# The router's product computed from transposed residual rows, between the w_o products

## What is computed

```python
x = x + gate1[:, None, :] * mix                          # mix = merged @ w_o
h = modulate(rms_norm(x, norm2_w[l]), shift2, scale2)    # (rms_norm(x) * w) * (1 + scale2) + shift2
ffn = moe_ffn(h, w_router[l], b_router[l], ...)
# in moe_ffn:
logits = (hf @ w_router + b_router).astype(jnp.float32)
top_vals, top_idx = lax.top_k(logits, TOP_K)
top_w = jax.nn.softmax(top_vals, axis=-1)
```

## Time and profile before

| | |
|---|---|
| time, three runs | 2203.03 us median (2201.9 to 2205.33) |
| time of the profiled execution | 2187.63 us |
| span of the profiled execution | 2185.8 us |
| TensorE busy | 2038.8 us (93%), 16673 instructions |
| VectorE busy | 810.2 us (37%) |
| ScalarE busy | 264.8 us (12%) |
| GpSimd busy | 155.1 us (7%) |
| mean granted TensorE clock | 0.971 |
| bytes moved | 563.70 MB, mean 258 GB/s |

### The profile page before, as it was taken

The page is one execution under the profiler, slowest core; times in us unless marked ns, Lnnn a source line. Parts: engine busy times, 40 slices in busy tenths (PEclk is TensorE's granted clock), DMA queues, the critical chain, the costliest instruction groups (busy, mean ns, idle before and its releaser), DMA issues.

```text
span 2185.8 us, 42419 instructions
## 1 busy us (share of the span) xinstructions
PE 2038.8 (93%) x16673; PEld 980.1 (45%) x16673; DVE 810.2 (37%) x1887; ACT 264.8 (12%) x585; POOL 155.1 (7%) x219
## 2 busy tenths in 40 slices
PE   6999999999979999998899999999999999999970
PEld 3564556455644444445343444444444444434430
DVE  1666886687663000043221221221221222222216
ACT  2122112112121000010100100100100100100000
POOL 0011111111110000011200000000000000000002
PEclk9999999999989999996999999999999999999995
DMA  9463333333124222436999999999999999999934
GB/s 316 124 187 119 113 116 93 94 115 96 53 73 144 77 77 67 138 136 240 305 413 404 407 407 402 407 411 405 403 410 403 404 406 406 409 405 403 410 136 179
DMA packets 199129, 563.70 MB, mean 258 GB/s; under 512 B 15181, under 2 KB 135025, under 8 KB 146357
## 3 DMA queue, kind: packets, MB, share of 16 engines
q1 hardware_dynamic: 176431, 528.12, 63.7%
q0 software_dynamic: 6624, 21.77, 2.9%
q10 hardware_dynamic: 16038, 13.32, 1.9%
HBM read 537.62 MB, written 25.54 MB: 258 GB/s over the span
## 4 chain that ended last, share of the span: by engine, by line
PE 48%; DVE 1%; POOL 1%; DMA 1%; issue 0%; ACTq 0%; ACT 0%; POOLq 0%; DVEq 0%
PE ps L1730 30%; PE ps L1752 16%; PE ps L1739 1%; PE ps L1717 1%; POOL ring L616 1%; DVE ring L1400 1%; POOL slot_tok L603 0%; DMA yT<-slot_tok 0%; DMA slot_tok<-tid,slotki 0%; DVE yT L1406 0%; DVE yT L1404 0%; DVE ring L1403 0%; ACTq L851 0%; ACT zs L896 0%; DVE ring L1397 0%
## 5 line engine op out<-in xcount | busy, mean ns | idle before, releaser
L1730 PE MATMUL ps<-ring,hT 128*32 128x512 f32 x6336 | 690.9, 595 | 1.1 <-ACT hT L865 1.1
L1417 PE MATMUL ps<-hT,ring 128*128 128x512 f32 x1008 | 440.4, 595 | 0.0
L1730 PEld LDWEIGHTS ps<-ring,hT 128*32 128x32 f32 x6336 | 203.4, 110 | 461.4 <-issue 457.5
L1752 PE MATMUL ps<-ring,seg 128*32 128x256 f32 x6336 | 348.7, 380 | 3.4 <-ACT seg L874 3.4
L1315 DVE TENSOR_TENSOR hT<-ps,bgu 128x512 f32<-128x512 f32 x99 | 67.9, 686 | 627.2 <-PE ps L1730 627.2
L1417 PEld LDWEIGHTS ps<-hT,ring 128*128 128x128 f32 x1008 | 191.1, 191 | 231.2 <-issue 230.6
L1752 PEld LDWEIGHTS ps<-ring,seg 128*32 128x32 f32 x6336 | 202.5, 110 | 137.5 <-ACT seg L874 3.6
L1018 DVE SCALAR_TENSOR_TENSOR c<-ring,pcur,c 128x512 f32<-128x512 f32 x232 | 155.5, 744 | 0.0
L857 ACT ACTIVATE mm<-hT 128x256 f32<-128x256 f32 x99 | 45.2, 457 | 694.8 <-DVE hT L1317 694.8
L1417 PE MATMUL ps<-yT,ring 128*128 128x512 f32 x256 | 111.2, 592 | 1.0 <-ACT yT L723 1.0
L1417 PE MATMUL ps<-ring,hT 128*128 128x256 f32 x512 | 111.8, 379 | 0.0
(11 more groups left out here) (258 smaller groups left out, 1327.6 us busy)
## 6 DMA issues: line engine op xcount, KB each, us to landing
ring<-in_w_gate_up_dram SPq DMA_DIRECT2D x264, 1024.0 KB, 8.8
ring<-in_w_down_dram SPq DMA_DIRECT2D x132, 1024.0 KB, 7.8
ring<-in_w_ada_dram SPq DMA_DIRECT2D x24, 1024.0 KB, 8.7
ring<-in_w_in_dram SPq DMA_DIRECT2D x48, 512.0 KB, 4.1
ring<-in_w_in_dram SPq DMA_DIRECT2D x16, 1024.0 KB, 5.4
item_rows<-zs ACTq DMA_DIRECT2D x132, 96.0 KB, 5.2
ring<-decay_rows SPq DMA_DIRECT2D x8, 1024.0 KB, 7.2
ring<-in_w_ssm_out_dram SPq DMA_DIRECT2D x8, 1024.0 KB, 5.5
```

The source lines that it names most:

```text
L1417: last = T.matmul(out_, lhs(k), rhs(k), start=(k == 0), stop=(k == n - 1))
L1730: last = T.matmul(ps[j * GT:(j + 1) * GT, g, :], xT[:, k, g * GT:(g + 1) * GT], gu[:, k, j * GUW:(j + 1) * GUW], start=(k == 0), stop=(k = ...
L1752: last = T.matmul(ps[j * GT:(j + 1) * GT, 3 + g // 2, (g % 2) * DW:(g % 2 + 1) * DW], hidT[:, k % 2, g, k // 2, :], dn[:, k, j * DW:(j + 1 ...
```

## The change

The router's product is no longer made from the normalised rows. The norm's weight and scale are per column of the width, so they are folded into the router's weights: `wra[k] = wr[k] * norm2_w * (1 + scale2)`. The shift gives a constant row, `shift2 @ wr`, which is added to `b_router` once. The factor `rstd` of each token is applied to the logits when VectorE reads them. So the transposes can take `x2` before its norm (`turn_x2`).

The product itself has the 32 router columns as stationary operand and 128 tokens moving, in four 32-column tiles (`router_parts`): tile j sums two of the eight blocks of the width. ScalarE copies the result to `lpart`, and one matmul with `sum4` (ones at a stride of 32) sums the four parts and turns them back to tokens by experts (`router_sum`). These steps and the rank products stand between the w_o products. The w_o products rotate over three banks in place of four.

For the folding, three loads (`wr`, moved from after the last `branch_a`, and two new ones of scale, shift and norm weight in rows, `mrows`) stand on SP's queue behind `load_branches(1)`. TensorE waits for them and transposes `mrows` behind `branch_b(0)`; VectorE builds `wra` and `wrs` behind `merge(0)`; TensorE computes the constant row behind the last branch product.

ScalarE's order changes: for each t it now does the two copies of the transposes, the copy of `lpart`, and then the Square; before, all four Squares stood ahead of all copies. VectorE's order is written out: residual 0, norm 0, residual 1, route 0, norm 1, residual 2, route 1, norm 2, residual 3, route 2, norm 3, route 3.

```diff
@@ SP
             load_branches(1)
+            sp.dma_start(wr, w_router[0].rearrange("(k p) n -> p k n", p=P)).then_inc(once_in, 16)
+            sp.dma_start(mrows[0:2 * KT, :], mod_rows[3 * KT:5 * KT, :]).then_inc(once_in, 16)
+            sp.dma_start(mrows[2 * KT:, :], norm2_w[0].rearrange("(k n) -> k n", n=P)).then_inc(once_in, 16)
             with sp.Fori(2, KT) as m:
...
             sp.dma_start(x2, x_v).then_inc(x2_in, 16)
-            sp.dma_start(wr, w_router[0].rearrange("(k p) n -> p k n", p=P)).then_inc(once_in, 16)
@@ ScalarE
             for t in range(TT):
+                act.wait_ge(x2T_pe, t + 1)
+                if t >= 2:
+                    act.wait_ge(lp_pe, t - 1)
+                for b in range(2):
+                    nc.scalar.activation(x2T[:, t % 2, 4 * b:4 * b + 4, :].rearrange("p k n -> p (k n)"), ps[:, 4 + b, :],
+                                         ACT.Copy).then_inc(x2T_ok, 1)
+                act.wait_ge(lp_pe, t + 1)
+                if t >= 2:
+                    act.wait_ge(lg_pe, t - 1)
+                nc.scalar.activation(lpart[:, t % 2, :], ps[:, 6, 0:P], ACT.Copy).then_inc(lp_ok, 1)
                 act.wait_ge(x2_ok, 4 * (t + 1))
                 if t:
                     act.wait_ge(sq_ok, TT + t)
                 nc.scalar.activation(orow, x2[:, t, :], ACT.Square, accum_out=ss[:, t:t + 1]).then_inc(sq_ok, 1)
-            for t in range(TT):
-                act.wait_ge(h2T_pe, t + 1)
-                if t >= 2:
-                    act.wait_ge(lg_pe, t - 1)
-                for b in range(2):
-                    nc.scalar.activation(h2T[:, t % 2, 4 * b:4 * b + 4, :].rearrange("p k n -> p (k n)"), ps[:, 4 + b, :],
-                                         ACT.Copy).then_inc(h2T_ok, 1)
@@ VectorE
             merge(0)
+            dve.wait_ge(prT_ok, 4)
+            V.tensor_copy(as2[:, 0:KT], ps[:, 6, 2 * KT:3 * KT]).then_inc(par_ok, 1)
+            V.tensor_copy(as2[:, KT:2 * KT], ps[:, 6, 0:KT]).then_inc(par_ok, 1)
+            dve.wait_ge(par_ok, 19)
+            V.scalar_tensor_tensor(as2[:, 0:KT], ps[:, 6, KT:2 * KT], 1.0, as2[:, 0:KT], ALU.add, ALU.mult).then_inc(par_ok, 1)
+            dve.wait_ge(par_ok, 20)
+            V.tensor_tensor(wra, wr, as2[:, 0:KT].unsqueeze(2).to_broadcast([P, KT, NE]), ALU.mult).then_inc(par_ok, 1)
+            V.tensor_tensor(wrs, wr, as2[:, KT:2 * KT].unsqueeze(2).to_broadcast([P, KT, NE]), ALU.mult).then_inc(par_ok, 1)
             with dve.Fori(1, KT) as m:
                 merge(m)
+            dve.wait_ge(prT_ok, 5)
+            V.tensor_tensor(brow[:, :], brow[:, :], ps[:, 6, 64:64 + NE], ALU.add).then_inc(par_ok, 1)
...
+            def route(t):
+
                 dve.wait_ge(lg_pe, t + 1)
-                link(V.tensor_tensor(lg[:, t, :], ps[:, LG_BANK[t], 0:NE], brow[:, :], ALU.add))
+                dve.wait_ge(rstd_ok, t + 2)
+                dve.wait_ge(par_ok, 23)
+                link(V.scalar_tensor_tensor(lg[:, t, :], logits(t), rstd[:, t:t + 1], brow[:, :], ALU.mult, ALU.add))
...
+            second_residual(0)
+            second_norm(0)
+            second_residual(1)
+            route(0)
+            second_norm(1)
+            second_residual(2)
+            route(1)
+            second_norm(2)
+            second_residual(3)
+            route(2)
+            second_norm(3)
+            route(3)
@@ TensorE
             branch_a(0, first=True)
             branch_b(0, first=True)
+            pe.wait_ge(once_in, 64)
+            T.transpose(ps[:, 6, 0:3 * KT], mrows, ident[0:3 * KT, 0:3 * KT]).then_inc(prT_ok, 1)
...
+            def turn_x2(t):
+                pe.wait_ge(x2_ok, 4 * (t + 1))
...
+            def router_parts(t):
+                pe.wait_ge(x2T_ok, 2 * t + 2)
...
+                for a in range(2):
+                    for j in range(4):
+                        last = T.matmul(ps[32 * j:32 * j + 32, 6, 0:P], wra[:, 2 * j + a, :], x2T[:, t % 2, 2 * j + a, :],
+                                        start=(a == 0), stop=(a == 1))
+                last.then_inc(lp_pe, 1)
+
+            def router_sum(t):
+                pe.wait_ge(lp_ok, t + 1)
...
+                T.matmul(logits(t), lpart[:, t % 2, :], sum4[:, :], start=True, stop=True).then_inc(lg_pe, 1)
...
+            pe.wait_ge(par_ok, 22)
+            for k in range(KT):
+                last = T.matmul(ps[:, 6, 64:64 + NE], ones[:, :], wrs[:, k, :], start=(k == 0), stop=(k == KT - 1))
+            last.then_inc(prT_ok, 1)
             pe.wait_ge(wo_in, 16)
             pe.wait_ge(mrg_ok, 3 * KT)
...
+            project_o(0, 0)
+            project_o(0, 1)
+            project_o(1, 0)
+            turn_x2(0)
+            project_o(1, 1)
+            router_parts(0)
+            project_o(2, 0)
+            router_sum(0)
+            turn_x2(1)
+            project_o(2, 1)
+            router_parts(1)
+            project_o(3, 0)
+            router_sum(1)
+            turn_x2(2)
+            rank_own(0)
+            project_o(3, 1)
+            router_parts(2)
+            rank_before(1)
+            rank_own(1)
+            router_sum(2)
+            turn_x2(3)
+            router_parts(3)
+            rank_before(2)
+            rank_own(2)
+            rank_before(3)
+            router_sum(3)
+            rank_own(3).then_inc(rank_pe, 1)
+            for j in range(TT):
+                last = T.matmul(ps[:, 4, 0:NE], ones[:, :], mask[:, j, :], start=(j == 0), stop=(j == TT - 1))
             last.then_inc(rank_pe, 1)
```

More of the change, by code:

```diff
@@ L232, in build @@
         wr = state[:, :, :].rearrange("p a b -> p (a b)").rearrange("p (k n) -> p k n", k=KT)
+        wra = ytmp[:, :].rearrange("p (k n) -> p k n", k=KT)
+        wrs = sqj[:, :].rearrange("p (k n) -> p k n", k=KT)
+        mrows = xb[0:3 * KT, 0, 0:P]
+        as2 = sb("as2", [P, 2 * KT])
+        sum4 = sb("sum4", [P, NE])
+        lpart = seg[:, :, 0, :]
         brow = sb("brow", [P, NE])
@@ L1221, in second_norm, with second_residual @@
                 V.tensor_tensor(h2[:, t, :], h2[:, t, :], s2row, ALU.add).then_inc(h2_ok, 1)
-            for t in range(TT):
+            def second_residual(t):
                 for hf in range(2):
                     n = 2 * t + hf
+                    cols = slice(hf * 512, (hf + 1) * 512)
                     dve.wait_ge(o_pe, n + 1)
@@ L1504, in _ @@
             for t in range(TT):
-                last = T.matmul(ps[:, 4, t * H:(t + 1) * H], dt_part[:, ch(t)], dt_sum, start=True, stop=True)
+                last = T.matmul(ps[:, 4, t * H:(t + 1) * H], dt_part[:, ch(t)], sum4[:, :], start=True, stop=True)
             last.then_inc(dtr_ok, 1)
@@ new lines, in router_sum, with rank, rank_before @@
+            def router_sum(t):
+                pe.wait_ge(lp_ok, t + 1)
+                if t:
+                    pe.wait_ge(mask_ok, t)
+                T.matmul(logits(t), lpart[:, t % 2, :], sum4[:, :], start=True, stop=True).then_inc(lg_pe, 1)
+            def rank(t):
+                return ps[:, 3, t * NE:(t + 1) * NE]
+            def rank_before(t):
+                for j in range(t):
+                    pe.wait_ge(mask_ok, j + 1)
+                    T.matmul(rank(t), ones[:, :], mask[:, j, :], start=(j == 0), stop=False)
@@ L1670, in _, with rank_own @@
+            def rank_own(t):
+                pe.wait_ge(mask_ok, t + 1)
+                return T.matmul(rank(t), before[:, :], mask[:, t, :], start=(t == 0), stop=True)
+            pe.wait_ge(par_ok, 22)
+            for k in range(KT):
+                last = T.matmul(ps[:, 6, 64:64 + NE], ones[:, :], wrs[:, k, :], start=(k == 0), stop=(k == KT - 1))
+            last.then_inc(prT_ok, 1)
             pe.wait_ge(wo_in, 16)
             pe.wait_ge(mrg_ok, 3 * KT)
[L1672 to L1677 removed]
@@ L1689, in rank @@
-            def rank(t):
-                return ps[:, 3, t * NE:(t + 1) * NE]
-            for t in range(TT):
-                for j in range(t):
-                    if t == 3 or j == t - 1:
-                        pe.wait_ge(mask_ok, j + 1)
-                    T.matmul(rank(t), ones[:, :], mask[:, j, :], start=(j == 0), stop=False)
-                if t == TT - 1:
-                    for j in range(t):
-                        T.matmul(ps[:, 4, 0:NE], ones[:, :], mask[:, j, :], start=(j == 0), stop=False)
-                pe.wait_ge(mask_ok, t + 1)
-                last = T.matmul(rank(t), before[:, :], mask[:, t, :], start=(t == 0), stop=True)
+            project_o(0, 0)
```

61 lines of the change are left out of this document (26 added, 35 removed).

## The result

The changed kernel takes 2212.59 us (median of six runs, 2211.73 to 2216.17) against 2202.26 for the kernel before (six runs, 2200.86 to 2205.33). The ratio is 1.0049 with an interval of 1.0036 to 1.0062: 10.3 us slower, between 7.9 and 13.7. The forecast was +4.2 us.

A forecast was written before the change was run, and what follows sets the result against it. TensorE was taken to bound the kernel from end to end, so the change could only move the expert loop's start. 7.8 - 4.3 + 0.7 = +4.2 us on the 2203.03 median gave 2207.2 us, range 2200 to 2214.

The forecast's parts named there:

- Step A: Merge stage: TensorE waits 5.4 us for the three loads, plus 0.2 transpose and 2.2 half clock; +7.8 us.
- rivals 3 and 4: Third: short load wait, clock holds, -0.1 us, chance 0.18. Fourth: clock falls in neither place, -2.7 us, chance 0.10.
- Step B: Router between the w_o products: half-clock products removed, serial chain through four engines added; -4.3 us.
- S+81.6: Forecast time at which the ranks are taken, counted in us from the start of the first w_o product.
- rival 1: Router chain: GpSimd's rstd held up by VectorE, 4.4 us more, total +8.6 us; chance 0.14.
- Step C: First gather of token rows, behind the router, slowed by the loads for expert 0; +0.7 us, upper bound +4.4.
- rival 2: First gather costs the loop's 8.7 us: +4.4 in place of +0.7, total +7.9 us; chance 0.12.
- The edits at nothing: Bias product, added VectorE operations, `wr` leaving its old place, `sum4` and a renamed semaphore: said to cost nothing.

The follow-up runs named there:

- loads_early: Changed kernel with the three parameter loads issued ahead of the load of `wo` and `load_branches(1)`; 2206.11 us, ratio 1.0007.
- wait_only: Kernel before plus only the three loads behind `load_branches(1)` and TensorE's wait and transpose of `mrows`, result unused; 2200.48 us, ratio 1.0036.
- square_first: Changed kernel with each Square on ScalarE ahead of the copies of its row tile; 2199.06 us, ratio 0.9985.
- weights_first: Changed kernel with the six loads for expert 0 ahead of the stores of the third and fourth normalised row tiles; 2205.5 us, ratio 1.0013.
- loads_late_before: Kernel before with the last six loads for expert 0 held until the ranks are there, beside the first gather; 2194.91 us, ratio 1.0009.
- router_alone: Changed kernel with loads_early and the four `dn` loads held behind the first gather, Square where the change put it; 2196.84 us, ratio 1.0003.
- dn_after_gather: Changed kernel with square_first and loads_early, and the four `dn` loads issued only after the first gather landed; 2179.08 us, ratio 0.9937.
- before_again: Kernel before, no edit, profiled a second time; 2203.14 us.
- all_three: Changed kernel with the edits of square_first, loads_early and weights_first together; 2184.0 us, ratio 0.9964.
- scatter_late: Kernel before with GpSimd's 16 indirect writes held until the hidden values of expert item 0 are there; 2206.05 us, ratio 1.0046.

## Why the prediction was right in part

*Step A (+7.8) held: +7.23.* The wait was 4.99 for 5.4, transpose and its start about 0.4 (the rest of the stage in loads_early) for 0.2, the half clock 1.8 for 2.2. loads_early takes it away and wait_only brings it alone. The value in the prediction for the short descriptors of `wr`, 1.3 us from the row, and the estimate from the Trainium skill of 0.5 (DMA: Bandwidth & Descriptors, "Why small descriptors are slow"), with waits of 5.4 and 4.6, lie on either side of 4.99; the runs don't separate them. The row of 1.20 us is not the router weights alone: its stretch moved 0.17 MB in 791 packets, of which 774 are short. In the changed kernel's trace the short packets, 1080 with the 1024 of `wr` among them, lie between 694.9 and 696.1 us, mixed with packets of the loads around them. The 4.99 us, with a granted clock of 0.50 behind them, also answer rivals 3 and 4: the wait was not short and the clock did fall.

*Step B (-4.3) held: -4.08.* Ranks were taken at 1009.77, S+82.0 for S+81.6. The waits were 0.57, 0.57 and 6.96 for 0.8, 0.8 and nearly 8, the chain through four engines 7.8 for 7.9, and 16 instructions of 32 columns 0.64 us for 0.5. No gap stands between the shapes in the rows, but the w_o products around them take 6.96 to 7.04 us from start to start in place of 6.87, so a drain of up to some 0.1 us for each change is not excluded. GpSimd took 0.19 + 0.54 in the chain (and 0.19 with 0.54 to 0.56 for the other three tiles): rival 1 fell. What the prediction did not draw from its own working: its chain is a fault of the order on ScalarE, and square_first is worth 12.5 us.

*Step C (+0.7) was mis-sized: +4.62.* The sentence "The nearest is the second: C = +0.7" failed. The second gather of the kernel before took 5.0 us; this one took 8.97, the loop's price, which was rival 2 and the upper bound. Its condition was met: the last load was issued at 1010.40, so 3.4 us before the gather, the DMA engines were at share 1.01 for all of the gather's time, and weights_first (5.78) and loads_late_before (9.94) switch the price off and on. The prediction's own working met it too: it had the loads run until about S+97 and the gather issued a few microseconds after S+81.6, yet gave this rival 0.12. Choosing the row by nearness in kind, a gather beside "weight loads", was the error. Full DMA engines alone do not make the difference: the second gather of the kernel before ran at a share of 0.96 and took 5.0. The gathers of 8.8 to 9.4 us in the seven traces that have one come after four or six loads of 1 MB issued at one go (all six, the last of them under 4 us ahead, or the four `dn` loads of router_alone and dn_after_gather some 17 us ahead, with more loads since), and the core moved 416 to 425 GB/s in their first 4.5 us; second gathers of 4.7 to 5.3 us had 355 to 375. That the amount queued at the issue is what counts is what this suggests; no run varies it alone.

*The edits at nothing.* They held. The bias product and the operations on VectorE show in no stage: P-S is 0.36 us longer in loads_early, where they all are and the wait is gone.

*What is left.* A + B + C by measure are +7.8 us, which is rival 2's +7.9. So the time lies in the range because the range took in a rival that was given a small chance, and not because the likeliest sum was right; that B came within 0.3 us and A within 0.6, term by term, is more than luck. Another 1.33 us lie in H-L, where the 96 instructions take 12.69 us against 11.27 in before_again, that is a longer stay at half clock, and -0.46 in T-H; I have no cause for either. The median says 10.3. The last 1.7 us are within the interval and not placed.

The forecast was made from a profile that lacked 13 us of a wait that both kernels' traces beside the runs contain (11 us net of what follows it). Adding the sum to the median of the runs, and not to the profile's time, kept that out of the number, but the wait matters for more than the level: where it is short, the slot table binds behind it, and what is saved ahead of it can be lost there (router_alone, with what is said there on the `dn` loads).

## What to carry to other kernels

Before a serial stage is moved between products, write down the order of each engine's list and put the work that others wait for first: here a Square behind a copy cost 12.5 us, three times what the move gained. A load that is waited for should be issued before the large ones and not behind them, and a gather on the critical path wants no burst of large loads just ahead of it; loads held back behind it are then in flight at the next gather, which has to be looked at too. When two profiles of one kernel differ by more than the effect under study, find the wait in which they differ before reading a saving from either.

## What the runs showed of the hardware

- A gather of 96 token rows landed in 4.3 to 4.6 us with few other transfers in flight (DMA share about 0.3 to 0.4), in 4.7 to 5.3 us with the DMA engines full (share 0.95 to 1.04) at 355 to 375 GB/s (6.5 us once, in all_three), and in 8.8 to 9.4 with them full at 416 to 425 GB/s, after 4 or 6 MB of loads had been issued at one go.
- After a gap of 4.99 us TensorE's granted clock was 0.50 in the stretch 698 to 700 us and 0.79 in the next 2 us, and 32 instructions took 1.8 us more than the 13.90 at full clock. Behind the gap of 6.96 us the eight transposes took 1.97 us, behind gaps of 0.57 us 1.09.
- VectorE stands idle 19.39 us for a "remote" release in before_again and 19.48 in the changed kernel, and its next operation starts 2.9 us after GpSimd's last indirect write has ended (issued 1054.07 for 0.95, so 1055.02, to 1057.91), though TensorE had finished the product it reads. In the traces of the other two groups the same wait on TensorE is 5.4 us with the same program. The cause is open; scatter_late was meant to show it and could not.
